# A two-layer hybrid backbone step on one core: weights of each stage's first units loaded and split a stage ahead, and a norm whose roots are taken on 128 columns

## What is computed

```python
h = _rmsnorm(x, lp['ffn1_norm']) * (1.0 + sc1) + sh1
x = x + 0.5 * gt1 * _swiglu(h, lp['ffn1_w_in'], lp['ffn1_w_out'])
h = _rmsnorm(x, lp['mix_norm']) * (1.0 + sc2) + sh2
m, s_gla, s_rw = _token_mix(h, lp, gla_s0, rw_s0, grid)
x = x + gt2 * m
h = _rmsnorm(x, lp['ffn2_norm']) * (1.0 + sc3) + sh3
x = x + 0.5 * gt3 * _swiglu(h, lp['ffn2_w_in'], lp['ffn2_w_out'])
```

## Time and profile before

| | |
|---|---|
| median of 3 runs | 2194.56 us (2189.89 to 2195.52) |
| profiled execution, its own time | 2195.91 us |
| its span in the trace | 2194.1 us |
| TensorE busy | 1941.8 us, 88% of the span |
| VectorE / ScalarE busy | 1017.9 us (46%) / 725.2 us (33%) |
| read from HBM | 259.08 MB |
| mean granted TensorE clock | 0.928 of full speed |

### The profile page before, as it was taken

One profiled execution on the slowest core, in us unless ns is written; L12 is line 12 of the kernel. 1 busy time (PEld: TensorE's weight loads), 2 busy tenths in 40 slices (PEclk: granted clock), 3 DMA queues, 4 the chain that ended last, 5 costly groups with the idle time before them and its releaser, 6 DMA issues. The chain is left out here.

```text
span 2194.1 us, 37567 instructions
## 1 busy us (share of the span) xinstructions
PE 1941.8 (88%) x16146; PEld 1757.4 (80%) x16146; DVE 1017.9 (46%) x1509; ACT 725.2 (33%) x1043; POOL 31.0 (1%) x62
## 2 busy tenths in 40 slices
PE   4999997997988968999979999799878796799996
PEld 1989996984655768999969999788657495799996
DVE  3333334655546554343344443464454755544434
ACT  3322324334242224332243332242431423433321
POOL 0000000001000000000000000000000100000000
PEclk8999998997979988999989999999878798899998
DMA  7665343314527032332323333332230502233232
GB/s 276 216 226 194 103 132 135 114 58 144 170 82 213 23 134 77 134 118 103 130 102 132 128 110 118 126 137 82 79 94 5 156 4 99 81 131 129 103 123 76
DMA packets 72612, 263.21 MB, mean 120 GB/s; under 512 B 9632, under 2 KB 10656, under 8 KB 56224
## 3 DMA queue, kind: packets, MB, share of 16 engines
q1 hardware_dynamic: 72480, 261.27, 35.0%
HBM read 259.08 MB, written 2.16 MB: 119 GB/s over the span
## 5 line engine op out<-in xcount | busy, mean ns | idle before, releaser
L149 PE MATMUL ps<-h_head,w_head 128*128 128x384 f32 x1952 | 672.0, 344 | 98.1 <-DVE h_rest L439 60.9
L149 PE MATMUL ps<-h_rest,w_head 128*128 128x384 f32 x1952 | 661.4, 339 | 0.0
L149 PE MATMUL ps<-h_head,w_rest 128*128 128x384 f32 x1952 | 661.2, 339 | 0.0
L358 DVE TENSOR_TENSOR w_rest<-w_raw,w_head 128x2048 fp32r<-128x2048 f32 (+1 forms) x186 | 383.7, 2063 | 347.7 <-ACT w_head L352 347.5
L149 PEld LDWEIGHTS ps<-h_head,w_head 128*128 128x128 f32 x1952 | 372.0, 191 | 135.4 <-DVE w_rest L358 83.7
L149 PEld LDWEIGHTS ps<-h_rest,w_head 128*128 128x128 f32 x1952 | 373.1, 191 | 0.2
L149 PEld LDWEIGHTS ps<-h_head,w_rest 128*128 128x128 f32 x1952 | 372.9, 191 | 0.0
L352 ACT ACTIVATE w_head<-w_raw 128x2048 fp32r<-128x2048 f32 (+1 forms) x186 | 321.0, 1726 | 156.1 <-PE ps L149 138.9
L149 PE MATMUL ps<-gu_head,w_head 128*128 128x384 f32 x704 | 237.0, 337 | 9.6 <-DVE gu_rest L602 7.2
L149 PE MATMUL ps<-gu_head,w_rest 128*128 128x384 f32 x704 | 237.0, 337 | 0.0
L149 PE MATMUL ps<-gu_rest,w_head 128*128 128x384 f32 x704 | 236.8, 336 | 0.0
(11 more groups left out here) (279 smaller groups left out, 1746.1 us busy)
## 6 DMA issues: line engine op xcount, KB each, us to landing
w_raw<-in_w_in SPq DMA_DIRECT2D x88, 1024.0 KB, 4.8
ada_raw<-in_ada_w SPq DMA_DIRECT2D x64, 1024.0 KB, 6.6
w_raw<-in_w_out SPq DMA_DIRECT2D x64, 704.0 KB, 4.1
w_raw<-in_mix_in SPq DMA_DIRECT2D x26, 1024.0 KB, 4.8
square<-in_ada_w SPq DMA_DIRECT2D x8, 1024.0 KB, 6.1
w_raw<-in_mix_out SPq DMA_DIRECT2D x8, 1024.0 KB, 4.9
hyena_const<-in_hconst SPq DMA_DIRECT2D x2, 1792.0 KB, 10.8
x<-in_x_in SPq DMA_DIRECT2D x1, 1536.0 KB, 11.8
```

Of the source, the lines that this page charges most:

```text
L149: return nc.tensor.matmul(out, lhsT, rhs, start=start, stop=stop)
L358: nc.vector.tensor_tensor(self.LO[:, j % 2, 0:cols], self.RAW[:, j % 2, 0:cols], self.HI[:, j % 2, 0:cols].bitcast(F32), ALU.subtract).the ...
```

## The change

- One `w_raw` of two slots for the whole program, shared by `Stream` and the mixer stages' `Ada`. Each stage loads the next stage's first two units into it, once its own last units have freed the slots (`load_ahead`, `load_next`).
- Where `w_head` and `w_rest` live on into the next stage (from the first ffn stage to the projection stage, and from layer 0's second ffn stage to layer 1's first), the next stage's first unit is also split there, between the last unit's waits (`split_next_head`, `split_next_rest`). Elsewhere the first unit is split in two halves, by contraction blocks.
- A stage's first unit is multiplied with the contraction blocks outside and the two output tiles inside (`by_tile`).
- The sum over channels is made by three matmuls of 32 output partitions, one for each 128 tokens, so that the 384 roots lie on 96 partitions x 128 columns; the last square goes in by a second group of three, not by an addition on VectorE. After root and reciprocal, three matmuls with one row of ones spread the values into three PSUM banks.
- The tile is multiplied by scale and reciprocal in one instruction for each token group (VectorE, from PSUM). The shift is added while the head is made (ScalarE) and again while the rest is made (VectorE).
- A root of one column, at the end of the stage before, brings the table of the root.
- The tail uses the same norm and sends the output in four parts. Layer 0 is no longer in a loop.

```diff
+        def total(src, start, stop):
+            for j in range(3):
+                last = mm(bank(7, 128, 32 * j, 32 * j + 32), cst("ones", 0, 32), src[:, 128 * j:128 * j + 128], start, stop)
+            return last
+        def spread_rows(inverse):
+            for j in range(3):
+                last = mm(bank(4 + j, 128), cst("ones", 0, 128, 32 * j, 32 * j + 1), inverse[32 * j:32 * j + 1, 0:128])
+            return last
+        def load_root_table():
+            nc.scalar.activation(WARM[:, :], EPS[:, 0:1], ACT.Sqrt)
...
             def root(self, act):
-                nc.scalar.activation(self.STD[:, :], bank(7, TOK), ACT.Sqrt, scale=1.0 / D_MODEL, bias=cst_eps)\
-                    .then_inc(self.std_done, 1)
+                root_of_total(self.STD).then_inc(self.std_done, 1)
+            def heads(self, act, split=None):
+                for dt in range(KT):
+                    if split and dt < 2:
+                        split(dt)
                     act.wait_ge(self.xn_done, dt + 2)
                     for s, (a, b) in enumerate(SEGS):
-                        last = nc.scalar.activation(self.SQ[:, dt, a:b], self.SQ[:, dt, a:b], ACT.Identity, scale=AFF[:, self.i, dt, s:s + 1],
-                                                    bias=MOD[:, (self.i + 1) % 3, 0, dt, s:s + 1])
-                    last.then_inc(self.sq_done, 1)
+                        last = nc.scalar.activation(self.HHI[:, dt, a:b], self.SQ[:, dt, a:b], ACT.Identity, bias=self.shift(dt, s))
+                    last.then_inc(self.head_done, 1)
...
+                nc.vector.reciprocal(self.RSTD[ROOTS, 0:128], self.STD[ROOTS, 0:128]).then_inc(self.xn_done, 1)
+                dve.wait_ge(self.spread_done, 1)
+                def scaled(dt):
+                    for s, (a, b) in enumerate(SEGS):
+                        last = nc.vector.scalar_tensor_tensor(by_128(self.SQ[:, dt, a:b]), by_128(X[:, dt, a:b]), AFF[:, self.i, dt, s:s + 1],
+                                                              spread_at(a, b), ALU.mult, ALU.mult)
+                    last.then_inc(self.xn_done, 1)
                 def rest(dt):
                     dve.wait_ge(self.head_done, dt + 1)
-                    nc.vector.tensor_tensor(self.HLO[:, dt, :], self.SQ[:, dt, :], self.HHI[:, dt, :].bitcast(F32), ALU.subtract)\
-                        .then_inc(self.rest_done, 1)
+                    for s, (a, b) in enumerate(SEGS):
+                        last = nc.vector.scalar_tensor_tensor(self.HLO[:, dt, a:b], self.SQ[:, dt, a:b], self.shift(dt, s),
+                                                              self.HHI[:, dt, a:b].bitcast(F32), ALU.add, ALU.subtract)
+                    last.then_inc(self.rest_done, 1)
                 for dt in range(KT):
-                    over_std(dt)
-                    if dt == 3 and first_split:
-                        first_split()
-                    if dt >= 3:
-                        rest(dt - 3)
-                for dt in range(KT - 3, KT):
+                    scaled(dt)
+                    if split and 1 <= dt <= 2:
+                        split(dt - 1)
+                    if dt >= 2:
+                        rest(dt - 2)
+                for dt in range(KT - 2, KT):
                     rest(dt)
+        def by_tile(tiles_outside):
+            if tiles_outside:
+                return [(t, kt) for kt in range(KT) for t in range(2)]
+            return [(t, kt) for t in range(2) for kt in range(KT)]
...
+            def load_next(self, sp, units, sources):
+                for u, (src, cols) in enumerate(sources):
+                    sp.wait_ge(self.rest_ready, units - 1 + u)
+                    load_ahead(sp, (units + u) % 2, cols, src)
+            def split_next_head(self, act, units):
+                act.wait_ge(NEXT[0], ahead[0])
+                act.wait_ge(self.used, units - 1)
+                for h in range(2):
+                    self.head((slice(None), 0, slice(h * 1024, h * 1024 + 1024))).then_inc(self.next_head, 1)
```

More of the change, by code:

```diff
@@ L178, in build, with load_ahead, split_buffers @@
         cst_eps, cst_lneps = EPS[:, 0:1], EPS[:, 1:2]
+        RAW = right(stack, "w_raw", [128, 2, 2048])
+        NEXT = [stack.enter_context(nc.semaphore(f"next{i}")) for i in range(2)]
+        ahead = [0, 0]
+        def load_ahead(sp, slot, cols, src):
+            ahead[slot] += 16
+            sp.dma_start(RAW[:, slot, 0:cols] if type(cols) is int else RAW[:, slot, :].rearrange("p (g n) -> p g n", g=ADA_J), src).then_inc(NEXT[slot], 16)
+        def split_buffers(scope):
+            return right(scope, "w_head", [128, 2, 2048], F32R), right(scope, "w_rest", [128, 2, 2048], F32R)
```

339 lines of the change are left out of this document (217 added, 122 removed).

## The result

The changed kernel takes 2135.65 us (median of 4 runs, 2131.5 to 2140.93) against 2192.79 for the kernel before, measured beside it: ratio 0.9741, interval 0.9712 to 0.9770. That is 57.1 us, where 58.1 were forecast. Its profiled execution took 2131.5 (span 2129.7), the shortest of its four runs, so stage by stage the two traces differ by more: 64.4 us of span.

A forecast was written before the change was run, and what follows sets the result against it. TensorE was taken as the busiest engine, so only its waits counted: norms 28.1, mix_out 12.8, GLA prefetches 11.2 and tail 6.0 sum to 58.1 us, from 2194.56 to 2136.5 us, range 2120 to 2154.

The forecast's parts named there:

- six norms: Norms of projection and both ffn stages: unit 1 ready 17.2 us behind the root, saving 28.1 us in all.
- mix_out's first unit: Start of the second ffn stages: TensorE starts 2.85 us after weights are there; gains 6.5 and 6.3, 12.8 us.
- GLA stages: First adaLN product loses its 5.62 us load wait and all shifts together, 2 x 5.6 = 11.2 us.
- tail: Last norm and output: 10.0 us in place of 16.06, a gain of 6.0 us.
- a step that makes the stream slower: In the norms, moving work to VectorE changes the pace from 1.28 us a tile (ScalarE) to 1.40 (VectorE).
- Barriers: no price: At stage ends, the early table load ends about 353.9, TensorE at 353.93, so the barrier doesn't move.
- Rival (f): At four barriers ScalarE comes late, a table load costing twice its 1.28 us, 1.3 us each: 2141.5 us; chance 0.05.
- (a): In the norms VectorE is dearer, 0.82 us a pair with PSUM operand, and spreads take 2.0: 2150 us; chance 0.14.
- (b): GLA stages keep their end as another chain replaces the wait, 11.2 us lost: 2148 us; chance 0.10.
- (c): TensorE's clock rises sooner in norms and GLA stages, 1 us at each of ten starts: 2126 us; chance 0.14.
- (d): Layer 0 outside a loop: eleven stage boundaries wait for instructions, at 7 us each 2213 us, slower than before; chance 0.02.
- (e): The prefetch does nothing, its wait in the projection stage being mostly covered by the reciprocal; no size given; chance 0.01.

The follow-up runs named there:

- roots384: Changed kernel with sum, root and reciprocal on 384 columns again, no spread, scaled tile reading SBUF (also called the SBUF run): 2153.03 us, ratio 0.9793.
- shift_undone: Changed kernel with scale and shift on ScalarE again, VectorE only dividing by the deviation and subtracting: 2147.74 us, ratio 0.9769.
- tile_off: Changed kernel with the first unit of each norm and of mix_out taking its two output tiles one after the other again: 2150.12 us, ratio 0.9798.
- mixo_noahead: Changed kernel with mix_out's first two weight units loaded behind the barrier of the second ffn stage again: 2149.12 us, ratio 0.9791.
- first_hold: Changed kernel with the first stage's two prefetch loads held back until its own eight adaLN loads have landed: 2137.69 us, ratio 0.9732.
- warm_off: Changed kernel without the one-column root at the stage ends, so the table load is behind the barrier again: 2134.47 us, ratio 0.9706.

## Why the prediction was right, point by point

The time was right by errors of opposite sign: the norms won more than forecast, the GLA stages and the first stage less. That the total came within 1.0 us was luck. Measured gains by term, in the profiled executions (norms from the barrier to unit 1's first matmul, those inside the second ffn stages from the last residual; mix_out from ScalarE's first instruction to the end of unit 0; the others by stage):

| term | forecast | measured |
|---|---|---|
| six norms | 28.1 | 7.0 + 7.7 + 6.8 + 5.1 + 5.2 + 3.1 = 34.9 |
| mix_out's first unit | 12.8 | 7.2 + 6.2 = 13.4 |
| GLA stages | 11.2 | 7.3 |
| tail | 6.0 | 6.7 |
| first stage | 0 | -2.2 |
| sum | 58.1 | 60.1 |

The other 4.3 us of the 64.4 are nearly all the clock: two low stretches in the second ffn stages of the kernel before (3.4) and one in layer 0's first ffn stage of the changed kernel (-1.7), and the two-pairs stages, whose granted clock went from 0.931 to 0.899 in layer 0 (2.2 longer) and from 0.879 to 0.919 in layer 1 (4.5 shorter). The median of four runs is then 4 us above the profiled execution, and the kernel before's 3 us below its own.

- **Norms: the mechanism right, three sizes too high.** Spread 0.80, not 1.4; root and first tile together 2.26, not 2.8; a pair 0.655, not 0.70, so a pace of 1.31. Unit 1 is ready at 15.8 in place of 17.2 (the terms add up to 17.1), 1.4 us a norm, about the surplus of the norms in the projection and second ffn stages (1.5, 2.2, 1.0 and 0.9). Against it, the sums brought the root forward by 1.2, not 1.4. The reciprocal (0.95) and the head of the last tile (0.8 with its wait, taken as 1.0) were as forecast. roots384 and shift_undone show what the narrow roots and the move to VectorE bring; the prediction called the latter a step that makes the stream slower. It does by 0.03 a tile (1.28 before, 1.31), and in layer 0's second ffn stage the shorter pipeline has the first matmul 0.8 and the last rest 1.1 sooner. That was an error of reasoning, hidden because both forms were costed from end to end.
- **The spread.** It takes 0.80 at a granted clock of 0.50. The six records start in two groups of three, each within 0.02 us (at 356.90 and 357.27), so the three row groups overlap; the row of eight, one after the other, would give 0.8 for six at the high clock and 1.4 where it took 1.88. The Trainium skill, TensorEngine Tiling (Array Packing), Key Properties, has different tiles work in parallel, and the trace agrees; of a drain at the change of mode the rows show nothing that could be told apart. It is 0.6 a norm less than forecast.
- **The second half of unit 0 leaves the path, unit 1's split comes next.** Shown by tile_off, by the two limits at 371.29 and 371.39, and by TensorE's waits of 0.74 and 0.83 for `w_rest` in the second ffn stages. In the other four norms both limits lie within 0.6 of each other.
- **mix_out.** First matmul 2.93 behind the barrier, 2.85 forecast. mixo_noahead gives the prefetch 5.8 of it in layer 0.
- **GLA: the step that failed.** "All shifts together" holds at the start and not to the end: 7.3 in place of 11.2. The first product loses its wait of 5.6, and the next matmul, which waits for `sig_w`, comes 5.4 and 5.2 sooner than before the change. Layer 1's stage gives 2.1 of that back: the same work now falls into the low clock (6.38 us in place of 3.93), and the fourth product's load is released by the second product. The forecast counted a removed wait in full and left out that the work behind it meets another clock. Layer 0's keeps 5.4 up to the fourth product; its end moves by itself by more than the gain.
- **Barriers: no price.** Wrong by a little. ScalarE, not TensorE, now ends the stages; at 354.59 against 353.68 it takes back 0.9 us of 1.28. The forecast had set ScalarE's end beside TensorE's of before, but the same change ends TensorE's sums 1.0 sooner behind the last square (0.6 in place of 1.6). The load itself costs its 1.28 there, with the one-column root 0.02 behind it. Rival (f), by the Trainium skill, ScalarE: Activation LUTs, What ACT_TABLE_LOAD costs, would have 1.38 more: the trace doesn't agree.
- **Gain in the first ffn stages.** It did outlast the root. In layer 1 it landed 2.43 behind its issue instead of 1.66 (why, with the last prefetch issued 10.8 us earlier, stays open), which the shorter rest of the norm made up for: 5.2, as forecast. In layer 0 the two prefetches queued ahead did not delay it (1.64); first_hold shows what they cost when they are issued shortly before it.
- **First stage.** No price was given and it cost 2.2. The seventh adaLN product comes 1.1 later, of which the shorter sums give back 0.6 (the eighth starts at 34.16, formerly 33.62); the last product and the row's turn took 1.94 + 1.88 in place of 1.06 + 1.06 in this execution, which is 1.7. The eight records of a product take 1.94 elsewhere at a granted 0.50, but the granted clock reads 1.00 here and up to 56 us, also where each matmul takes 0.52 as at the low level: in this stretch of the trace the level is told by the durations alone. warm_off had 1.19 and 1.06, and its stage is 0.6 longer than before's. first_hold excludes the prefetch as the cause of the later products. What it is (the loads follow one another at 2.70 us a product where it was 2.55) stays open; another chip or another place of the buffers weren't told apart.
- **Tail.** 9.4 in place of 10.0: first tile 2.34 behind the root (2.8 forecast), eight operations in 4.29 (4.5), and 2.76 from their end to the last output (2.7).
- **Rivals.** (a) is out by the SBUF run. (b) is 1.0 us in layer 1 and 0.4 in layer 0; what else the GLA stages lost is the clock. (c) is there in layer 0's mix_out, 0.8 us in unit 0 (10.2 against 11.0), not in layer 1's (10.1 in both), and in layer 1's GLA stage it went the other way. (d), (e) didn't happen.

## What to carry to other kernels

When a prefetch takes a wait away, follow the same instructions through the stage, before and after, counted from its start: in layer 1's GLA stage the shift was 5.7 us at the product, 4.7 at the next matmul, 3.0 at the next load and 2.9 at the end. The wait that is removed is an upper bound. When a pass moves from one engine to another, count the depth of the pipeline at its first and last tile, not only the pace. A warm-up instruction in front of a barrier hides its load only if its engine isn't the last to arrive there, and it is lost where something else behind the barrier is waited for. And before two stages are compared, compare the granted clock in both.

## What the runs showed of the hardware

- One and the same wait of 2.4 us on TensorE has 3.4 us at a granted 0.50 with it or none, in executions of nearly the same program: 37 and 19 of 56. Layer 0's GLA stage, with unchanged code, took 122.0 to 130.8 us over twelve profiles; in one of 130.8 the window 545 to 560 ran at a granted 0.54, in the changed kernel's at 0.85. Swings of this size are enough for the 9 us between the changed kernel's own runs, and gains below 5 us were seen in distances only.
- Three products with weights of one row and 128 columns, in fp32 six records, took 0.80 us at a granted clock of 0.50 and 0.50 us at 1.00 (first_hold's layer 1). Two times three column groups of 32 x 128 for the sums took 0.42 and 0.40 at 1.00, 0.65 and 0.64 at 0.50; the full-width form 1.65 and 1.49 at 0.50.
- A SCALAR_TENSOR_TENSOR of VectorE with one operand in PSUM, spread over three banks, costs no more than with all in SBUF (three pairs 2.04 and 2.06; 344 and 348 ns for 128 columns, 477 and 481 for 256).
- The gain, a load of 12 KB, landed 1.64 us behind its issue in layer 0, 2.96 with two loads of 1 MB issued some 4 us before it.
